# Dense units that run their three token blocks abreast, instead of one after the other

## What is computed

```
for i in range(2):
    xn = rmsnorm(x); z = xn @ w_in[i]            # 8 x 256 mixer columns and 4 x 1024 gate columns
    branches = mixers A, B, C, D of z            # short conv, wide conv, pooling, gated chunks
    mixed = sum(sigmoid(z_gate[b]) * (branch[b] @ w_branch[i, b]) for b in range(4))
    x = x + mixed @ w_out[i]
    xn = rmsnorm(x)
    if i == 0: x = x + (silu(xn @ w_gate) * (xn @ w_up)) @ w_down      # dense, 2816 hidden columns
    else:      x = x + top-2-of-8 experts of the same form, 3584 hidden columns each
    x = x + sigmoid(rmsnorm(x) @ ple_w_gate[i]) * (p[i] @ ple_w_proj[i])
y = rmsnorm(x)
```

## Time and profile before

| | |
|---|---|
| median of 3 runs | 5047.31 us |
| the profiled execution | 5047.06 us, of it 5045.4 us span |
| TensorE matmul busy | 4927.9 us (98%), 33245 matmuls |
| TensorE weight loads | 4872.2 us (97%), 33246 loads |
| VectorE busy | 3235.8 us (64%) |
| ScalarE busy | 1745.6 us (35%) |
| GpSimd busy | 301.5 us (6%) |
| mean granted clock of TensorE | 0.987 of full speed |

### The profile page before, as it was taken

How to read it: one execution, slowest core, us unless ns; L and a number is a source line. 1 busy time by engine, 2 the same in 40 slices (tenths; PEclk the granted TensorE clock), 3 DMA queues, 4 the chain that set the end, 5 groups by cost and what they waited for, 6 DMA issues and landing times.

```text
span 5045.4 us, 87414 instructions
## 1 busy us (share of the span) xinstructions
PE 4927.9 (98%) x33245; PEld 4872.2 (97%) x33246; DVE 3235.8 (64%) x5250; ACT 1745.6 (35%) x2666; POOL 301.5 (6%) x441
## 2 busy tenths in 40 slices
PE   8999999999999999999979999999999999999988
PEld 8999999999998999999979999999999999999988
DVE  4667656444446656776557777666667887876655
ACT  3323322111113433233234444333334444443333
POOL 2000002111112000000020000000000000000030
PEclk9999999999999999999989999999999999999999
DMA  3111111111111111111035554444445555654431
GB/s 107 45 47 41 43 39 43 51 42 42 50 42 44 42 47 51 48 42 44 29 100 196 178 175 162 162 144 157 153 152 200 189 194 181 202 187 153 145 131 43
DMA packets 397853, 521.94 MB, mean 103 GB/s; under 512 B 13192, under 2 KB 353654, under 8 KB 397512
## 3 DMA queue, kind: packets, MB, share of 16 engines
q1 hardware_dynamic: 358320, 459.63, 27.6%
q10 hardware_dynamic: 29272, 33.08, 1.9%
q0 software_dynamic: 9920, 24.85, 1.7%
HBM read 494.91 MB, written 22.60 MB: 103 GB/s over the span
## 4 chain that ended last, share of the span: by engine, by line
PE 84%; issue 8%; DVE 4%; DMA 1%; ACT 1%; DVEq 0%; POOL 0%; ACTq 0%; SPq 0%; POOLq 0%
PE PS L705 20%; PE PS L707 20%; PE PS L706 20%; PE PS L817 5%; PE PS L818 5%; PE PS L819 5%; PE PS L753 1%; PE PS L754 1%; PE PS L755 1%; PE PS L1243 1%; DMA WRAW<-in_moe_w_gate 0%; DVE WLO L1702 0%; ACT WHI L1301 0%; DVE XLO L1722 0%; PE PS L880 0%
## 5 line engine op out<-in xcount | busy, mean ns | idle before, releaser
L1702 DVE TENSOR_TENSOR WLO<-WRAW,WHI 128x1024 fp32r<-128x1024 f32 x866 | 1060.7, 1226 | 417.9 <-ACT WHI L1301 298.2
L705 PE MATMUL PS<-XHI,WHI 128*128 128x384 f32 (+1 forms) x3648 | 1199.2, 329 | 14.4 <-DVE XLO L1959 8.2
L1301 ACT ACTIVATE WHI<-WRAW 128x1024 fp32r<-128x1024 f32 x866 | 899.2, 1051 | 858.9 <-PE PS L819 601.5
L707 PE MATMUL PS<-XHI,WLO 128*128 128x384 f32 (+1 forms) x3648 | 1194.9, 328 | 0.0
L706 PE MATMUL PS<-XLO,WHI 128*128 128x384 f32 (+1 forms) x3648 | 1193.8, 327 | 0.0
L705 PE MATMUL PS<-XSH,WHI 128*128 128x232 f32 (+6 forms) x3584 | 1059.8, 296 | 15.1 <-DVEq L2460 10.0
L707 PE MATMUL PS<-XSH,WLO 128*128 128x232 f32 (+6 forms) x3584 | 1055.9, 295 | 0.0
L706 PE MATMUL PS<-XSL,WHI 128*128 128x232 f32 (+6 forms) x3584 | 1055.7, 295 | 0.0
L705 PEld LDWEIGHTS PS<-XHI,WHI 128*128 128x128 f32 x3648 | 688.7, 189 | 16.6 <-issue 8.9
L705 PEld LDWEIGHTS PS<-XSH,WHI 128*128 128x128 f32 x3584 | 679.8, 190 | 17.4 <-DVEq L2460 13.8
L706 PEld LDWEIGHTS PS<-XLO,WHI 128*128 128x128 f32 x3648 | 688.5, 189 | 0.9
(11 more groups left out here) (409 smaller groups left out, 5803.1 us busy)
## 6 DMA issues: line engine op xcount, KB each, us to landing
WRAW<-in_moe_w_gate SPq DMA_DIRECT2D x112, 1024.0 KB, 5.0
WRAW<-in_moe_w_up SPq DMA_DIRECT2D x112, 1024.0 KB, 5.0
WRAW<-in_moe_w_down SPq DMA_DIRECT2D x112, 1024.0 KB, 4.9
WRAW<-in_w_in SPq DMA_DIRECT2D x48, 1024.0 KB, 5.1
WRAW<-in_ffn_w_gate SPq DMA_DIRECT2D x11, 1024.0 KB, 5.3
WRAW<-in_ffn_w_up SPq DMA_DIRECT2D x11, 1024.0 KB, 5.3
WRAW<-in_ffn_w_down SPq DMA_DIRECT2D x11, 1024.0 KB, 4.9
expert_rows<-YT ACTq DMA_DIRECT2D x18, 512.0 KB, 3.8
```

The costliest lines, as they stand in the source:

```text
L705: pe.matmul(PS[:, bank, 0:n], wh, hi(k), start=(k == 0), stop=False)
L707: ins = pe.matmul(PS[:, bank, 0:n], wl, hi(k), start=False, stop=(k == KC - 1))
L1301: act.activation(WHI[halves.n % HL][:], raw_view(tile % RAW, half, kind), ACT.Copy).then_inc(halves.next(), 1)
L1702: v.do(dve.tensor_tensor(WLO[s][:], raw_view(conv.n // 2 % RAW, conv.n % 2, kind), WHI[s][:].bitcast(F32), ALU.subtract), conv)
```

## The change

Units with neither `splits` nor `between` no longer go through `blocks_of`. They run `blocks_abreast`: one wait at the unit's start until at most the last three products are unevicted, then three banks at once. For each of the 8 contraction blocks come six matmuls with the high weights (high and low activations of each of the three token blocks), then three with the low weights. The three products of the unit end with its last three matmuls. VectorE's, ScalarE's, GpSimd's and SyncE's programs stay as they are.

```diff
+        def blocks_abreast(HI, LO):
+
+            wait(pe, S["evicted"], q.before(BANKS - len(BLOCKS)))
+            slot = unit.n % HL
+            banks = [(q.n + j) % BANKS for j in range(len(BLOCKS))]
+            for k in range(KC):
+                wh, wl = WHI[slot][:, k, :], WLO[slot][:, k, :]
+                for b, (t0, n) in zip(banks, BLOCKS):
+                    pe.matmul(PS[:, b, 0:n], wh, HI[:, k, t0:t0 + n], start=(k == 0), stop=False)
+                    pe.matmul(PS[:, b, 0:n], wh, LO[:, k, t0:t0 + n], start=False, stop=False)
+                for b, (t0, n) in zip(banks, BLOCKS):
+                    ins = pe.matmul(PS[:, b, 0:n], wl, HI[:, k, t0:t0 + n], start=False, stop=(k == KC - 1))
+                    if k == KC - 1:
+                        ins.then_inc(q.next(), 1)
+
         def column_unit(HI, LO, splits=None, between=()):
 
             use()
-            blocks_of(HI, LO, splits, between)
+            if splits is None and not between:
+                blocks_abreast(HI, LO)
+            else:
+                blocks_of(HI, LO, splits, between)
             unit.n += 1
```

## The result

The changed kernel takes 5115.81 us (median of 4 runs, 5113.49 to 5120.0) against 5046.61 us for the kernel before (a fourth run of it joined the three above). The ratio is 1.0136, with a 95% interval of 1.0124 to 1.0148: 69 us slower. The prediction was 5104 us, its range 5070 to 5125.

The account below looks back on a forecast made before the run. TensorE, busy for 98% of the span, was taken to bound the kernel. DN stalls 31, clock falls 12 and other joints 3.5 + 3.7 + 4 + 3 made 57 us on 5047.06: 5104 us, range 5070 to 5125.

Parts of the forecast that it names:

- The bound: Whole kernel: TensorE's own work bounds it; the dense stage has no wait to remove, so removed waits are worth nothing.
- Rival 1: TensorE's matmul steps get shorter, 76 us less, 5028 us with the stalls; chance 0.05.
- rival 2: VectorE absorbs the piled-up chains, so no change: 5047 to 5057 us; chance 0.05.
- The DN term: Ten DN steps after a GU: TensorE waits 3.1 us each for VectorE's late first ACC, 31 us.
- The clock: Behind DN's stalls TensorE falls to half clock, 7 times in 10 at 1.7 us: 12 us, bounds 0 and 17.
- Rival 3: Stalls without falls of the clock: 5092 us, or 5086 with 2.5 us per DN; chance 0.25.
- The other joints: Outside DN, VectorE chains piled up behind the last changed unit delay TensorE: 3.5 + 3.7 + 4 + 3 us.
- w_out: End of w_out: VectorE's late chain costs 3.5 us in layer 0 and 3.7 us in layer 1.
- the chunk products: VectorE's first eviction there comes 2.0 us later behind the last mixer block, in 2 layers: 4 us.
- the state transposes: VectorE's copies for them come 3.7 us later against 2.3 us slack: 1.4 to 1.6 us, x 2, 3 us.
- The steps: TensorE's matmuls in the 76 changed units: new order set to cost zero, bounds +-11 us.
- Rival 4: TensorE's steps get longer from bank changes or jumping operands: 5115 us, or 5138 at the higher price; chance 0.10.

Follow-up runs that it names:

- the run on orders: Changed kernel, but the four units of each dense GU step use four different matmul orders, the last one the old order; one execution, 5084.02 us.
- the late conversion: Changed kernel, all 76 units abreast, with VectorE's weight conversion in DN moved behind the first six additions to ACC; 5094.25 us, ratio 1.0088.
- m = 1, 2, 4: Changed kernel with each abreast unit's last m contraction blocks done token block by token block; 5103.32, 5076.18 and 5051.50 us in that order.
- the run on them: Changed kernel with all dense units back in the old order, the 33 others (19 mixer, 14 w_out) abreast; 5072.53 us, ratio 1.0049.
- the run with every direct joint in the old order: Changed kernel with the units directly ahead of something that leans on VectorE put back, 54 units abreast; 5059.46 us, ratio 1.0021.
- the run with only the joint: Kernel before, with only the second up unit of each GU step, ahead of DN, abreast (11 units); 5093.92 us, ratio 1.0084.

## Why the prediction was right, and where its sum was off

**The bound.** Right: TensorE had no wait in the dense stage to lose, and the removed waits brought nothing. Rival 1 (cheaper steps) falls by the 33246 loads and by the run on orders; rival 2 (VectorE absorbs it) by the ten waits.

**The DN term, 31 us.** Right in place, count and cause; the runs with the late conversion and with m = 1, 2, 4 show the cause, not only the trace. Per DN it was 3.1 us; measured are 2.69 us at the seventh product and 0.24 at the sixth, and a DN without a fall is 27.3 us long against 23.99 (75.1 less 47.8 of GU), so 3.3 us each, 33 us in all. The rest beyond the idle time is there because idle time begins only when the last matmul has drained (0.16 us behind its step) and the first one after a wait takes longer (0.28 us to the next start, where there is no fall, and not 0.18).

**The clock, 12 us.** I took 7 falls in 10 at 1.7 us each. There were 6, at 1.5 us (among DN steps with the same wait at the sixth product, 28.6 to 29.0 us with a fall against 27.3 and 27.4 without): 9 us. Rival 3, no falls, is what the late conversion and m = 2 made of it.

**The other joints, 14 us.** This is the term that was sized wrong: 25 us by the run on them, of which 1.7 is growth of steps (19 units of XHI at 0.09). Term by term: the idle time was sized well. w_out had 3.5 and 3.7 us (the first is 833.5 - 830.1 = 3.4), measured 3.1 idle in layer 0 and 4.1 us by the shift of that stage in layer 1; the chunk products 2.0, measured 2.12 - 0.14 = 2.0 us each; the state transposes 1.5, measured 1.04. Two things were left out. First, I priced falls of the clock only in DN, and put them at other joints into the range alone; behind the w_out joint of layer 0 they cost 3.4 us. Second, the waits for PWL in the gate projections (1.41 + 1.41 + 1.03 = 3.9 us; the profile's row for them went from 2.7 to 6.5 us): VectorE's program has a step of its own there on which TensorE leans, and I had looked at the places behind a unit only, and not at the places within the gate projection that follows it. These terms make 3.1 + 3.4 + 4.1 + 4.0 + 2.1 + 3.9 + 1.7 = 22.3 of the 25 us. In the profiled execution of after the clock also fell behind the wait of 2.12 us at the chunk products of layer 0 (0.82 and 0.75 in the two windows of 4 us from 124 on, 1.7 us); behind the same wait in layer 1, and in both layers of the run on these joints, it did not. Another 3 us lie there in the mixer stage of layer 1, where the clock stays low for longer behind a wait of 8.2 us that stands in both kernels; the runs differ there among themselves, and that part stays open.

**The steps, 0 us with a bound of 11.** They grew by 0.011 us per contraction block in units of XHI (GU is 47.79 us long against 47.44, so 0.09 us for a unit) and not at all in w_out, where a contraction block is 1.500 us in either order. 62 units of XHI make 5.4 us.

**The sum again.** 33 + 9 + (25 - 1.7) + 5.4 = 71 us, against 69.2 measured. The 25 in it carries the interval of its run, 16 to 33 us, so that the sum closes to 2 us is better than the runs can vouch for. Rival 4 had the measured number (5115) by adding 11 us of longer steps to the forecast; the steps are 5.4 us, so the agreement is chance.

## What to carry to other kernels

Products that run abreast also end together. Before interleaving them, walk through the program of the engine that evicts them, from the common end to the next thing that the matmul engine needs from it: that walk gave 3.1 us per place, and 2.9 were measured. It must go on past the next unit (a late chain reached over a whole unit of 12 us and still cost 0.8 us behind it), take in every small step that is queued behind the evictions, and price a fall of the clock at every place where it gives an idle stretch, with a share and not as certain. The Trainium skill, "Perfetto Trace Analysis", section "Matmuls", says that independent matmul groups should rotate through PSUM banks so that the evacuation of one overlaps the next group's matmuls; the kernel rotates in both versions, and the runs with m = 1, 2 and 4 show that the distance between the ends decides, not the rotation alone.

## What the runs showed of the hardware

Idle stretches of TensorE of the same length are not always followed by the lower clock: of ten at 2.69 us, six were, in two kernels; of ten between 2.25 and 2.68 us (m = 1), six; of ten between 1.29 and 1.82 us (m = 2) and of ten between 1.05 and 1.15 us (late conversion), none. But a short stretch is no guarantee: in the run with every direct joint in the old order the clock fell behind the one of 1.20 us at the sum of squares. And at the start of w_out, where three or four waits of 0.4 to 0.8 us follow each other 1.2 us apart in both kernels, it fell in layer 1 and not in layer 0 before, and in layer 0 and not in layer 1 after. So the clock made a longer wait dearer than its length, by 1.5 us where it fell in the changed kernel and by up to 2.7 us in the run with only the joint: between m = 1 and m = 2 the waits in DN lose 24.6 - 15.1 = 9.5 us and the falls 9 us, of 27 us that the kernel gains (the rest at the other joints).

At the full clock the mean step of 384 columns is 0.174 us in a unit of XHI in the old order and 0.177 us in one of MHI in the same order, and a contraction block of XHI takes 1.480 to 1.501 us in four orders. The differences follow neither the number of bank changes nor how often a weight tile is repeated: with three changes and two matmuls in a row on one tile it is 1.501 us, with nine and six 1.500, with six and six 1.495.
